# Order of the last chunks, last units and first units in a two-block transformer kernel

## The chip, the cores and the metric

The kernel runs on one core of a Trainium2 chip. TensorE (PE) multiplies matrices into PSUM; VectorE (DVE), ScalarE (ACT) and GpSimd (POOL) compute on SBUF, the first two on PSUM too; SyncE (SP) here only issues DMAs. Each engine runs its own instructions in order, and they wait for one another by semaphores. The metric is the time on the device in microseconds (us), the median of the runs.

## The reference

Two transformer blocks over 1024 tokens of width 1024, all in float32. The first has a Fourier branch and softmax attention. The second, on which the change bears, has stick-breaking attention, a causal convolution, gates and a gated feed-forward part:

```python
h = rms_norm(x, norm_mix_pre)
proj = h @ w_in                                  # values v are 512 of its columns
...
x = x + rms_norm(merged @ w_out, norm_mix_post)  # the second output projection
h = rms_norm(x, norm_ffn_pre)
u = causal_dwconv(h @ w_up, conv_ffn_w)          # 1024 -> 2 x 2816
a, g = split(u)
f = (gelu(g) * a) @ w_down                       # 2816 -> 1024, the down projection
out = x + rms_norm(f, norm_ffn_post)
```

## The kernel before

Precision comes from splitting each float32 operand into a high part in the fast fp32r format and a low part, the rest. The helper three (L672 to L676) issues the three matmuls high x high, high x low and low x high, each 128x128 by 512 columns.

**Weights.** They come in chunks of 128x1024, in the order of the constants C_V2, C_OUT2, C_UP, C_DOWN. SyncE loads a chunk into one of two staging slots (w_staging). GpSimd splits it (split, L559 to L570: two operations for the high part, L566 and L567, one for the low part, L569) into one of the four slots of w_ring, and raises w_split. It may do so once the chunk that held the slot four chunks before is used; TensorE raises w_used for that behind its last matmul with a chunk.

**Token-major units** (tm_units, L688). A unit is one tile of 128 tokens by 512 columns; it runs over chunks times two steps of the contraction, 24 matmuls in all for four chunks. The first lead units are interleaved chunk by chunk, the last two as well, the others run one after another. before(u) adds waits, after(u) adds the eight transposes of a normalised tile. For the values (T_V2) lead is 1, and behind units 0 to 3 tiles 4 to 7 of the block's input are transposed. For the second half of the second output projection (T_OUT2 + TT) lead is 2, and behind unit u stand the transposes of tile u - 3. ScalarE copies the high part out of PSUM (L1560), VectorE subtracts to get the low part (L1917) and raises nt_free. Then the up projection starts with the first token half: it waits for the tiles 0 to 3, and for the copies of all units (tm_free).

**Down projection.** The gated product (ffn_mid, FFT) has 22 feature tiles (FT), one for each weight chunk. All eight banks of PSUM hold the sums of four token tiles by 1024 columns, so the tokens are done in two halves of four tiles, and each half runs over its 22 chunks. For each chunk ScalarE makes the high part of 128x512 (mid_hi, L1819), VectorE the low part (mid_lo, L2378), into one of two slots of ffn_split (FS); a slot is free once the chunk two before is used. TensorE's down() does six matmuls for each token tile, 24 a chunk. In the last chunk each tile raises dn_mm (the last one w_used), ScalarE and VectorE copy its 1024 columns to ffn_out (Y2; L1863 and L2412), and half 1 may use the banks again. Then finish() does the root mean square, for each tile: square (L1832) and a first guess of the inverse root on ScalarE, its refinement (L1891 to L1894), scaling by gain (L2389) and the addition of the residual (L2392) on VectorE; ScalarE stores the tile (L1837) and loads the residual of the tile two on (L1827). For half 0 these steps stand between mid_hi and mid_lo of half 1's chunks 2 to 7, in both engines' order. For half 1 they come behind the copies of all four tiles.

Of the kernel before, what the change touches and what calls it, by code (L numbers as in the profile page):

```python
# [22 lines left out]
F32R = mybir.dt.float32r  # L23
# [4 lines left out]
P = 128  # L28
D = 1024
# [229 lines left out]
def two_block_kernel(nc, a, const, scratch, out):  # L259
    ctx = ExitStack()  # L260
    with ctx:
# [133 lines left out]
        FS = at("ffn_split", [P, 2, 2, N_TOK], R1, F32R)[:, :, :, 0:FW]  # L395
        Y2 = at("ffn_out", [P, 4, D], R1 + 4096)
# [266 lines left out]
        def _(pe):  # L663
# [24 lines left out]
            def tm_units(t0, units, c0, chunks, ncols, stat, before=None, after=None, follows=False, lead=1):  # L688
# [326 lines left out]
            tm_units(T_V2, TT, C_V2, 4, FW, a2_stat, follows=True,  # L1015
# [134 lines left out]
            tm_units(T_OUT2 + TT, TT, C_OUT2 + 4, 4, FW, mr_stat, follows=True, lead=2,  # L1150
# [39 lines left out]
            for half in range(2):  # L1190
                def down(j, s, first=False, last=False):
# [5 lines left out]
                    for t in ((2, 3, 0, 1) if first and not half else range(4)):  # L1197
# [6 lines left out]
                        for g in range(2):  # L1204
                            ins = three(PB[:, 2 * t + g, :], sh, sl, WR[:, r, 0, FW * g:FW * (g + 1)],
                                        WR[:, r, 1, FW * g:FW * (g + 1)], first, last)
                        if last and t < 3:
                            ins.then_inc(S["dn_mm"], 1)
# [7 lines left out]
                for s in range(FT - 4, FT):  # L1216
                    down(s, s, last=s == FT - 1)
# [3 lines left out]
        def _(act):  # L1221
# [625 lines left out]
            for half in range(2):  # L1847
                if half:
                    mid_hi(1, 1, 1)
                    for s in range(6):  # L1850
                        if s < 5:
                            finish(0, s)
                        mid_hi(1, s + 2, s % 2)
                with act.Fori(4 if half else 1, FT // 2) as i:
                    for s in range(2):
                        mid_hi(half, i * 2 + s, s)
                if half:
                    act.wait_ge(S["f_stored"], 64)
                else:
                    mid_hi(1, 0, 0)  # L1860
                for t in range(4):
                    down_ready(act, half, t)
                    act.activation(Y2[:, t, 0:FW], PB[:, 2 * t, :], ACT.Copy).then_inc(S["dn_ya"], 1)  # L1863
                act.wait_ge(S["dn_ya"], 4 * half + 4)
                act.wait_ge(S["dn_yv"], 4 * half + 4)
            for s in range(5):
                finish(1, s)

            act.wait_ge(S["f_stored"], 16 * TT)
# [3 lines left out]
        def _(v):  # L1873
# [519 lines left out]

            v.wait_ge(S["gains3_in"], 16)
            v.wait_ge(S["up_f"], FT + 1)
            for half in range(2):
                if half:
                    mid_lo(1, 1, 1)
                    for s in range(6):
                        if 1 <= s < 5:  # L2400
                            finish(0, s - 1)
                        mid_lo(1, s + 2, s % 2)
                with v.Fori(4 if half else 1, FT // 2) as i:
                    for s in range(2):
                        mid_lo(half, i * 2 + s, s)
# [106 lines left out]
```

## Time and profile before

| | us |
|---|---|
| runs before | 2164.91, 2169.05, 2169.08; median 2169.05 |
| profiled execution | 2165.13 |
| its span, first to last instruction | 2162.9 |
| TensorE busy | 2091.7 (97%) |
| VectorE busy | 1086.4 (50%) |
| ScalarE busy | 828.9 (38%) |
| GpSimd busy | 747.1 (35%) |
| mean granted clock of TensorE | 0.991 of 2.4 GHz |

The span is what the trace covers; the 2.2 us around it belong to the execution's time. Busy shares are means over all stages. The down projection runs from about 1890 to 2144, the second output projection ends at 1388, the values units run from 611 to 664. A row of the timeline is one instruction with its start, its length, its engine and line, what it writes and reads, and in brackets how long the engine had been idle before it and who ended that.

### The profile page before, as it was taken

To read this page: it belongs to the slowest core of one execution; us is meant where nothing else is said; L and a number is where in the kernel's file an instruction comes from. 1 tells how busy PE (TensorE), PEld (TensorE's weight loads), DVE (VectorE), ACT (ScalarE), POOL (GpSimd) and SP (SyncE) were. 2 spreads that over 40 slices of the span, in tenths; PEclk is the share of its full clock that TensorE was granted. 3 is DMA by queue.
4 is the path that set the end of the run, shared out by engine and by line. 5 is a ranking of instruction groups with operands and counts; after the bars stand their busy time and mean duration, and the time that the engine had idled before them with its cause. 6 is when DMAs were issued, how large, how long until landed. Compare 5 with 4: busy or idle time off the path is not lost.

```text
span 2162.9 us, 27982 instructions
## 1 busy us (share of the span) xinstructions
PE 2091.7 (97%) x10634; PEld 1742.7 (81%) x10634; DVE 1086.4 (50%) x1576; ACT 828.9 (38%) x1482; POOL 747.1 (35%) x661
## 2 busy tenths in 40 slices
PE   8999999999999999999999999999999999999996
PEld 7988889998877787778877888778888888878785
DVE  6565678885261666667576650722223222221613
ACT  4342279995242555645455321522212221111212
POOL 2532422222234222223221444043333333367672
PEclk9999999999999999999999999999999999999998
DMA  5211210101322111112112533321111111132432
GB/s 168 61 49 68 69 57 11 47 11 50 112 99 59 51 63 54 63 43 74 52 47 106 193 126 108 137 59 49 48 48 48 48 40 47 48 117 97 155 98 78
DMA packets 144683, 159.91 MB, mean 74 GB/s; under 512 B 6939, under 2 KB 112951, under 8 KB 144583
## 3 DMA queue, kind: packets, MB, share of 16 engines
q1 hardware_dynamic: 121319, 97.45, 14.8%
q10 hardware_dynamic: 23264, 61.10, 8.0%
q8 instruction: 67, 1.10, 0.2%
q14 instruction: 33, 0.27, 0.0%
HBM read 129.16 MB, written 29.36 MB: 73 GB/s over the span
## 4 chain that ended last, share of the span: by engine, by line
PE 84%; DVE 7%; issue 5%; ACT 2%; POOL 1%; DMA 1%; ACTq 0%; DVEq 0%; POOLq 0%
PE psum L674 18%; PE psum L676 17%; PE psum L675 17%; PE psum L1035 15%; PE psum L931 3%; PE psum L943 3%; PE psum L1072 1%; PE psum L962 1%; PE psum L963 1%; PE psum L964 1%; DVE softplus_part L2231 1%; PE psum L1056 1%; PE psum L684 1%; PE psum L1057 1%; PE psum L1089 1%
## 5 line engine op out<-in xcount | busy, mean ns | idle before, releaser
L566 POOL TENSOR_TENSOR w_ring<-w_staging,zero 128x8 fp32r<-128x8 f32 x172 | 43.4, 252 | 1187.3 <-PE psum L676 705.2
L569 POOL TENSOR_TENSOR w_ring<-w_staging,w_ring 128x1024 fp32r<-128x1024 f32 (+1 forms) x172 | 445.7, 2591 | 14.4
L1035 PE MATMUL psum<-h,w_ring 128*128 128x512 f32 x1728 | 434.1, 401 | 0.7 <-ACT v L1565 0.7
L1035 PEld LDWEIGHTS psum<-h,w_ring 128*128 128x128 f32 x1728 | 317.5, 190 | 67.9 <-ACT v L1565 1.1
L674 PE MATMUL psum<-ffn_in,w_ring 128*128 128x512 f32 x672 | 265.4, 395 | 0.0
L676 PE MATMUL psum<-ffn_in,w_ring 128*128 128x512 f32 x672 | 264.2, 393 | 0.0
L675 PE MATMUL psum<-ffn_in,w_ring 128*128 128x512 f32 x672 | 263.8, 393 | 0.0
L2364 DVE SCALAR_TENSOR_TENSOR up_buf<-psum,vectors,up_buf 128x1023 f32<-128x1023 f32 x44 | 56.4, 1283 | 309.8 <-ACT up_buf L1808 309.8
L567 POOL TENSOR_SCALAR w_ring<-w_staging 128x1016 fp32r<-128x1016 f32 (+1 forms) x172 | 184.3, 1071 | 0.0
L1808 ACT ACTIVATE up_buf<-psum,vectors 128x1024 f32<-128x1024 f32 x44 | 49.2, 1117 | 268.0 <-PE psum L676 267.9
L676 PEld LDWEIGHTS psum<-ffn_in,w_ring 128*128 128x128 f32 x672 | 126.0, 188 | 30.5
L675 PEld LDWEIGHTS psum<-ffn_in,w_ring 128*128 128x128 f32 x672 | 126.3, 188 | 29.3
L674 PEld LDWEIGHTS psum<-ffn_in,w_ring 128*128 128x128 f32 x672 | 126.0, 188 | 29.0
L674 PE MATMUL psum<-w_ring,ffn_split 128*128 128x512 f32 x352 | 140.7, 400 | 4.9 <-DVE ffn_split L2378 4.9
L676 PE MATMUL psum<-w_ring,ffn_split 128*128 128x512 f32 x352 | 139.9, 397 | 0.0
L675 PE MATMUL psum<-w_ring,ffn_split 128*128 128x512 f32 x352 | 139.7, 397 | 0.0
L2378 DVE TENSOR_TENSOR ffn_split<-ffn_mid,ffn_split 128x512 fp32r<-128x512 f32 x44 | 45.0, 1025 | 174.2 <-ACT ffn_split L1819 169.3
L2243 DVE TENSOR_TENSOR stick_w_t<-psum,stick_w_t 128x512 fp32r<-128x512 f32 (+3 forms) x96 | 53.4, 556 | 111.9 <-ACT stick_w_t L1642 111.9
L1819 ACT ACTIVATE ffn_split<-ffn_mid 128x512 fp32r (+1 forms) x44 | 27.7, 632 | 202.3 <-PE psum L676 184.6
L2231 DVE TENSOR_TENSOR_SCAN softplus_part<-one,softplus 128x128 f32<-128x128 f32 (+7 forms) x64 | 97.6, 1525 | 2.2
L1642 ACT ACTIVATE stick_w_t<-psum 128x512 fp32r<-128x512 f32 (+3 forms) x96 | 47.1, 491 | 130.5 <-PE psum L1072 129.3
L1520 ACT ACTIVATE probs<-psum,minus_max 128x348 f32<-128x348 f32 x192 | 91.6, 551 | 2.3 <-DVE minus_max L2157 1.9
(286 smaller groups left out, 4543.2 us busy)
## 6 DMA issues: line engine op xcount, KB each, us to landing
w_staging<-in_w_in SPq DMA_DIRECT2D x58, 512.0 KB, 3.8
w_staging<-in_w_up SPq DMA_DIRECT2D x44, 512.0 KB, 3.8
w_staging<-in_w_down SPq DMA_DIRECT2D x44, 512.0 KB, 3.3
w_staging<-in_w_out SPq DMA_DIRECT2D x16, 512.0 KB, 3.8
scratch_gates<-gate_out ACTq DMA_DIRECT2D x32, 256.0 KB, 2.3
merge_gates<-scratch_gates ACTq DMA_DIRECT2D x16, 512.0 KB, 4.5
x_again<-scratch_x ACTq DMA_DIRECT2D x16, 512.0 KB, 4.4
x_again<-in_x ACTq DMA_DIRECT2D x16, 256.0 KB, 2.7
```

The source lines that it names most:

```text
L567: pool.tensor_scalar(hi[:, 0:w], WS[:, s, 0:w], 1.0, 0.0, ALU.mult, ALU.add).then_inc(S["w_hi"], 1)
L569: pool.tensor_tensor(lo[:, 0:width], WS[:, s, 0:width], plain(hi[:, 0:width]), ALU.subtract).then_inc(S["w_split"], 1)
L674: pe.matmul(dst, sh, mh, start=first, stop=False)
L675: pe.matmul(dst, sh, ml, start=False, stop=False)
L676: return pe.matmul(dst, sl, mh, start=False, stop=last)
L931: ins = pe.matmul(PB[:, b, 0:KPART], QS[:, h, P * t:P * t + P], k2[:, h // GROUP, KPART * b:KPART * (b + 1)], start=x == 0, stop=x == 1)
L943: ins = pe.transpose(PB[0:rows, 3 + g, P * (kt % 4):P * (kt % 4) + P], PR[:, i % 2, first:first + rows], IDENT[:, :])
L1035: ins = pe.matmul(mix_bank(h), (sl if x == 2 else sh)[:, P * k:P * k + P], ml if x == 1 else mh, start=m == 0, stop=m == UNIT // 2 - 1)
L1520: act.activation(PR[:, i % 2, KPART * b:KPART * (b + 1)], PB[:, b, 0:KPART], ACT.Exp, bias=NB[:, i % 2:i % 2 + 1], scale=-1.0).then_inc(S[ ...
L2231: link(v.tensor_tensor_scan(ZL[:, i % 2, n - 1::-1], ONE[:, 0:1].broadcast_to([P, n]), ZS[:, i % 3, n - 1::-1], 0.0, ALU.mult, ALU.add))
L2243: v.tensor_tensor(WT[:, 1, 4 * g:4 * g + w, cols], PB[:, 4, 0:P * w].rearrange("p (k n) -> p k n", n=P), plain(WT[:, 0, 4 * g:4 * g + w, c ...
L2364: v.scalar_tensor_tensor(out=UB[:, g, 1:N_TOK], in0=up[:, 0:N_TOK - 1], scalar=w1, in1=UB[:, g, 1:N_TOK], op0=ALU.mult, op1=ALU.add).then_ ...
```

## The change

In tm_units a flag paired=False runs the last two units one after another too; the second half of the second output projection uses it. The values units get lead=2.

In the down projection the last four chunks (18 to 21) of each half run tile by tile: all four chunks for token tile 0, then for tile 1, and so on. Their high and low parts go to a buffer of their own, ffn_split_last (FSL), with a slot for each of the four. dn_mm is raised after each tile's four chunks; w_used of the four chunks only within tile 3. The copies and finish() of half 0 stand tile by tile (copy, then finish), and chunks 0 and 1 of half 1 have their parts made before the first of them. In half 1 nothing is copied: ScalarE squares straight from PSUM (pair(t)), VectorE scales straight from PSUM, and the last tile is scaled, added and stored in two halves of 512 columns.

```diff
+        FSL = at("ffn_split_last", [P, 4, 2, FW], R1 + 12288, F32R)
...
-            def tm_units(t0, units, c0, chunks, ncols, stat, before=None, after=None, follows=False, lead=1):
+            def tm_units(t0, units, c0, chunks, ncols, stat, before=None, after=None, follows=False, lead=1,
+                         paired=True):
...
-                for u in range(lead, units - 2):
+                for u in range(lead, units - 2 if paired else units):
                     for j in range(chunks):
                         part(u, j)
                     if after is not None:
                         after(u)
+                if not paired:
+                    return
...
-            tm_units(T_V2, TT, C_V2, 4, FW, a2_stat, follows=True,
+            tm_units(T_V2, TT, C_V2, 4, FW, a2_stat, follows=True, lead=2,
...
-            tm_units(T_OUT2 + TT, TT, C_OUT2 + 4, 4, FW, mr_stat, follows=True, lead=2,
+            tm_units(T_OUT2 + TT, TT, C_OUT2 + 4, 4, FW, mr_stat, follows=True, lead=2, paired=False,
...
-                for s in range(FT - 4, FT):
-                    down(s, s, last=s == FT - 1)
+                c = C_DOWN + FT * half
+                for t in range(4):
+                    for s in range(FT - 4, FT):
+                        if t == 0:
+                            pe.wait_ge(S["w_split"], c + s + 1)
+                            pe.wait_ge(S["dn_lo"], FT * half + s + 1)
+                        r = (c + s) % 4
+                        sh, sl = (FSL[:, s - FT + 4, x, P * t:P * t + P] for x in range(2))
+                        for g in range(2):
+                            ins = three(PB[:, 2 * t + g, :], sh, sl, WR[:, r, 0, FW * g:FW * (g + 1)],
+                                        WR[:, r, 1, FW * g:FW * (g + 1)], False, s == FT - 1)
+                        if t == 3:
+                            ins.then_inc(S["w_used"], 1)
+                        elif s == FT - 1:
+                            ins.then_inc(S["dn_mm"], 1)
...
             def mid_hi(half, j, s):
-                if half or not isinstance(j, int) or j >= 2:
+                if not isinstance(j, int):
                     act.wait_ge(S["w_used"], j + (C_DOWN + FT * half - 1))
+                elif half:
+                    act.wait_ge(S["w_used"], C_DOWN + FT - 4 + j - 1)
...
+            def last_hi(half, j):
+                if half:
+                    act.wait_ge(S["w_used"], C_DOWN + FT)
+                act.activation(FSL[:, j - FT + 4, 0, :], FFT[:, j, FW * half:FW * half + FW], ACT.Copy).then_inc(S["dn_hi"], 1)
...
+            with act.Fori(1, FT // 2 - 2) as i:
+                for s in range(2):
+                    mid_hi(0, i * 2 + s, s)
+            for j in range(FT - 4, FT):
+                last_hi(0, j)
+            mid_hi(1, 0, 0)
+            mid_hi(1, 1, 1)
+            for t in range(4):
+                down_ready(act, 0, t)
+                act.activation(Y2[:, t, 0:FW], PB[:, 2 * t, :], ACT.Copy).then_inc(S["dn_ya"], 1)
+                act.wait_ge(S["dn_ya"], t + 1)
+                act.wait_ge(S["dn_yv"], t + 1)
+                finish(0, t)
+            finish(0, 4)
...
+            for t in range(4):
+                down_ready(act, 1, t)
+                link(act.activation(JUNK3[:, :], pair(t), ACT.Square, accum_out=SS[:, t:t + 1]))
+                guess(P, t, 1, 1.0 / D, False)
+                if t:
+                    m = 4 + t - 1
+                    act.wait_ge(S["f_out"], m + 1)
+                    act.dma_start(out[0, P * m:P * m + P, :], Y2[:, t - 1, :]).then_inc(S["f_stored"], 16)
+                    if m + 2 < TT:
+                        load_x2(m + 2)
+            for h in range(2):
+                cols = slice(FW * h, FW * h + FW)
+                act.wait_ge(S["f_out"], TT + h)
+                act.dma_start(out[0, N_TOK - P:N_TOK, cols], Y2[:, 3, cols]).then_inc(S["f_stored"], 16)
...
+            with v.Fori(1, FT // 2 - 2) as i:
+                for s in range(2):
+                    mid_lo(0, i * 2 + s, s)
+            for j in range(FT - 4, FT):
+                last_lo(0, j)
+            mid_lo(1, 0, 0)
+            mid_lo(1, 1, 1)
+            for t in range(4):
+                down_ready(v, 0, t)
+                v.tensor_copy(Y2[:, t, FW:D], PB[:, 2 * t + 1, :]).then_inc(S["dn_yv"], 1)
+                finish(0, t)
...
+            v.wait_ge(S["f_stored"], 64)
+            for t in range(4):
+                m = 4 + t
+                refine(P, t, 1, 1.0 / D, RSTD)
+                for h in range(2 if t == 3 else 1):
+                    cols = slice(FW * h, FW * h + FW) if t == 3 else slice(0, D)
+                    link(v.scalar_tensor_tensor(out=Y2[:, t, cols], in0=pair(t)[:, cols], scalar=RSTD[:, t:t + 1],
+                                                in1=GL[:, cols], op0=ALU.mult, op1=ALU.mult))
+                    if h == 0:
+                        v.wait_ge(S[f"xf_in{m % 2}"], 16 * (m // 2 + 1))
+                    v.tensor_tensor(Y2[:, t, cols], Y2[:, t, cols], XF[:, m % 2, cols], ALU.add).then_inc(S["f_out"], 1)
```

The flag last of down() and the loops that stood there before on ScalarE and VectorE, described above, are taken out.

## Rows read from the trace of the kernel before

**Rows 1.** Page, busy time: us, share of the span, instructions.

```profile
PE 2091.7 (97%) x10634; PEld 1742.7 (81%) x10634; DVE 1086.4 (50%) x1576; ACT 828.9 (38%) x1482; POOL 747.1 (35%) x661
```

**Rows 2.** Timeline, values units: start us, us, engine, operation, [idle before, releaser].

```profile
615.63 0.50 PE L674 MATMUL psum<-w_ring,h 128*128 128x512 f32 x1 [1.75 <-POOL w_ring L569]
...
616.83 2.35 POOL L569 TENSOR_TENSOR w_ring<-w_staging,w_ring 128x1024 fp32r<-128x1024 f32 x1
...
619.23 0.50 PE L674 MATMUL psum<-w_ring,h 128*128 128x512 f32 x1 [1.93 <-POOL w_ring L569]
...
621.97 1.22 DVE L1917 TENSOR_TENSOR h<-psum,h 128x1024 fp32r<-128x1024 f32 x1
```

**Rows 3.** Timeline, end of the second output projection.

```profile
1386.49 0.60 ACT L1768 ACTIVATE mix_out<-psum 128x512 f32<-128x512 f32 x1 [5.21 <-PE psum L676]
...
1387.70 1.91 PE L684 MATMUL psum<-ident,xn 128*128 128x128 f32 x16
...
1389.89 1.22 DVE L1917 TENSOR_TENSOR ffn_in<-psum,ffn_in 128x1024 fp32r<-128x1024 f32 x1 [4.18 <-ACT ffn_in L1560]
...
1391.95 0.47 PE L674 MATMUL psum<-ffn_in,w_side 128*128 128x512 f32 x1 [2.34 <-DVE ffn_in L1917]
```

**Rows 4.** Stretches: busy us by engine, granted clock (PEclk), DMA share, GB/s.

```profile
616.00:621.00 5.00, 3.07 (x15) 2.18 (x14) 4.93 (x5) 0.11 (x1) 3.09 (x2) 1.00 0.44 126
...
1393.40:1396.80 3.40, 3.40 (x10) 2.60 (x9) 3.40 (x3) 2.26 (x5) 0.00 (x0) 0.51 0.39 153
...
2042.00:2045.40 3.40, 3.40 (x10) 2.62 (x9) 2.32 (x2) 0.00 (x0) 0.00 (x0) 0.50 0.54 192
```

**Rows 5.** Timeline, boundary of the down projection's halves.

```profile
2014.29 0.40 PE L674 MATMUL psum<-w_ring,ffn_split 128*128 128x512 f32 x1
...
2033.65 3.34 DVE L2392 TENSOR_TENSOR ffn_out<-ffn_out,x_again 128x1024 f32<-128x1024 f32 x1
...
2038.56 2.70 DVE L2378 TENSOR_TENSOR ffn_split<-ffn_mid,ffn_split 128x512 fp32r<-128x512 f32 x1 [1.57 <-ACT ffn_split L1819]
...
2041.32 0.50 PE L674 MATMUL psum<-w_ring,ffn_split 128*128 128x512 f32 x1 [4.31 <-DVE ffn_split L2378]
```

**Rows 6.** Timeline, VectorE beside back-to-back splits of weights.

```profile
607.65 3.51 DVE L2198 SCALAR_TENSOR_TENSOR h<-h,rstd_x,final_gain 128x1024 f32<-128x1024 f32 x1
...
607.69 2.39 POOL L569 TENSOR_TENSOR w_ring<-w_staging,w_ring 128x1024 fp32r<-128x1024 f32 x1
```

**Rows 7.** Timeline, steady chunks of the down projection, half 1.

```profile
2110.63 0.63 ACT L1819 ACTIVATE ffn_split<-ffn_mid 128x512 fp32r x1 [5.03 <-PE psum L676]
...
2116.13 0.20 POOL L566 TENSOR_TENSOR w_ring<-w_staging,zero 128x8 fp32r<-128x8 f32 x1 [1.58 <-PE psum L676]
...
2117.43 2.74 POOL L569 TENSOR_TENSOR w_ring<-w_staging,w_ring 128x1024 fp32r<-128x1024 f32 x1
...
2133.08 0.63 ACT L1819 ACTIVATE ffn_split<-ffn_mid 128x512 fp32r x1 [5.03 <-PE psum L676]
```

**Rows 8.** Timeline, the tail behind the last matmul.

```profile
2143.76 0.40 PE L676 MATMUL psum<-w_ring,ffn_split 128*128 128x512 f32 x1
...
2144.19 0.69 DVE L2412 COPY ffn_out<-psum 128x512 f32<-128x512 f32 x1 [0.72 <-PE psum L676]
...
2146.63 0.15 DVE L1891 TENSOR_SCALAR mean<-sumsq 128x1 f32<-128x1 f32 x1 [1.74 <-ACT rsqrt_guess L1249]
...
2147.27 1.28 DVE L2389 SCALAR_TENSOR_TENSOR ffn_out<-ffn_out,rstd,last_gain 128x1024 f32<-128x1024 f32 x1
...
2158.62 1.23 DVE L2392 TENSOR_TENSOR ffn_out<-ffn_out,x_again 128x1024 f32<-128x1024 f32 x1 [0.78 <-DMA x_again<-scratch_x]
```

**Rows 9.** DMA view, issues: count, KB each, median us to landing.

```profile
scratch_gates<-gate_out ACTq DMA_DIRECT2D x32, 256.0 KB, 2.3
...
x_again<-scratch_x ACTq DMA_DIRECT2D x16, 512.0 KB, 4.4
...
out<-ffn_out ACTq DMA_DIRECT2D x8, 512.0 KB, 3.0
```

More of the change, by code:

```diff
@@ L1190, in _, with down @@
             for half in range(2):
-                def down(j, s, first=False, last=False):
+                def down(j, s, first=False):
                     c = C_DOWN + FT * half
@@ L1205, in down @@
                             ins = three(PB[:, 2 * t + g, :], sh, sl, WR[:, r, 0, FW * g:FW * (g + 1)],
-                                        WR[:, r, 1, FW * g:FW * (g + 1)], first, last)
-                        if last and t < 3:
-                            ins.then_inc(S["dn_mm"], 1)
+                                        WR[:, r, 1, FW * g:FW * (g + 1)], first, False)
                     ins.then_inc(S["w_used"], 1)
@@ L1846, in _ @@
             load_x2(1)
[L1847 to L1865, printed above, removed]
@@ L1866, in _ @@
-            for s in range(5):
-                finish(1, s)
-            act.wait_ge(S["f_stored"], 16 * TT)
+            with act.Fori(1, FT // 2 - 2) as i:
[11 more added lines that the diff above has]
+                finish(0, t)
@@ new lines, in _ @@
+            finish(0, 4)
+            with act.Fori(1, FT // 2 - 2) as i:
+                for s in range(2):
+                    mid_hi(1, i * 2 + s, s)
+            for j in range(FT - 4, FT):
+                last_hi(1, j)
+            for t in range(4):
[8 more added lines that the diff above has]
+                        load_x2(m + 2)
@@ L1872, in _ @@
+            for h in range(2):
+                cols = slice(FW * h, FW * h + FW)
+                act.wait_ge(S["f_out"], TT + h)
+                act.dma_start(out[0, N_TOK - P:N_TOK, cols], Y2[:, 3, cols]).then_inc(S["f_stored"], 16)
+            act.wait_ge(S["f_stored"], 16 * (TT + 1))
         @block.vector
@@ L2392, in finish, with last_lo @@
                 v.tensor_tensor(Y2[:, s, :], Y2[:, s, :], XF[:, m % 2, :], ALU.add).then_inc(S["f_out"], 1)
+            def last_lo(half, j):
+                v.wait_ge(S["dn_hi"], FT * half + j + 1)
+                v.tensor_tensor(FSL[:, j - FT + 4, 1, :], FFT[:, j, FW * half:FW * half + FW],
+                                plain(FSL[:, j - FT + 4, 0, :]), ALU.subtract).then_inc(S["dn_lo"], 1)
             v.wait_ge(S["gains3_in"], 16)
             v.wait_ge(S["up_f"], FT + 1)
[L2396 to L2405, printed above, removed]
-                if half:
-                    v.wait_ge(S["f_stored"], 64)
-                else:
-                    mid_lo(1, 0, 0)
-                for t in range(4):
-                    down_ready(v, half, t)
-                    v.tensor_copy(Y2[:, t, FW:D], PB[:, 2 * t + 1, :]).then_inc(S["dn_yv"], 1)
@@ L2413, in _ @@
-            for s in range(4):
-                finish(1, s)
+            with v.Fori(1, FT // 2 - 2) as i:
+                for s in range(2):
+                    mid_lo(0, i * 2 + s, s)
+            for j in range(FT - 4, FT):
+                last_lo(0, j)
[5 more added lines that the diff above has]
+                finish(0, t)
@@ new lines, in _ @@
+            with v.Fori(1, FT // 2 - 2) as i:
+                for s in range(2):
+                    mid_lo(1, i * 2 + s, s)
+            for j in range(FT - 4, FT):
+                last_lo(1, j)
+            v.wait_ge(S["f_stored"], 64)
[9 more added lines that the diff above has]
+                    v.tensor_tensor(Y2[:, t, cols], Y2[:, t, cols], XF[:, m % 2, cols], ALU.add).then_inc(S["f_out"], 1)
```

## The prediction

> **What bounds the kernel now.** Read the page first: TensorE is busy 97% of the span and at full clock nearly throughout [rows 1]. So an edit pays only where TensorE stands still, or after its last matmul. The timeline of TensorE, searched for starts more than 0.26 us apart, shows where: two waits in the first values unit [rows 2], one ahead of the up projection [rows 3], one in the second half of the down projection [rows 5], and the tail [rows 8]. The change touches all four.
>
> A unit of 24 matmuls, or one chunk of the down projection, takes 5.61 us: four chunks lie between the two hi copies of [rows 7], (2133.08 - 2110.63) / 4. Six matmuls take 1.40 us.
>
> **Values units.** Unit 0 reads its four weight chunks as GpSimd splits them and waits for the third and fourth, 1.75 and 1.93 us; with the matmul that starts late behind each wait, it ends 4.2 us later than a unit without waits [rows 2]. With lead=2 each chunk serves two units, 2.8 us instead of 1.4, so the fourth chunk is wanted at about 619.3; its split ends at 616.83 + 2.35 = 619.18. Both waits go. What is late next: transposes of tiles 4 and 5 now stand together behind units 0 and 1, at 622.2, and tile 5 needs VectorE's subtraction for tile 3, which starts at 621.97 and ends at 623.19: 0.2 to 0.4 us of wait. GpSimd and VectorE aren't moved by this edit, and the units' last slots are released as before. **Gain 3.8** (3.4 to 4.1).
>
> **Second output projection.** Units 6 and 7 interleaved end 1.4 us apart, the copy of unit 6 starts at 1386.49, the transposes of tiles 3 and 4 at 1387.70, and the up projection waits 2.34 us for VectorE's half of tile 3 [rows 3]. The stretch behind the wait runs at a granted clock of 0.51, that is 1.2 GHz [rows 4]: some eight matmuls at 0.43 instead of 0.23 us, 1.5 us. In sequence unit 6 ends 4.2 us earlier (5.61 - 1.40), tile 3 is transposed ahead of unit 7, and its subtraction, at 1389.89 today, comes before unit 7 is through, at 1387.70 plus the 0.9 us of eight transposes. The other condition, the copy of unit 7, starts 0.43 us behind the unit's last matmul as in [rows 8], takes 0.6 and ends near 1389.7, just as the transposes of tile 4 do. So the up projection starts near 1389.9 instead of 1391.95, and at 2.4 GHz: 2.05 + 1.5. The slots of the four chunks are released later by up to 4 us, but the next split waits for the last normalised tile (the test at C_UP + 2 in GpSimd's loop) anyway. The next wait, in front of the second token half, hangs on TensorE's own transposes and moves along. **Gain 3.6** (2.0 if the clock falls anyway, 4.0 at most).
>
> **The tail.** Now: last matmul starts at 2143.76, both engines copy at 2144.19, the mean is read at 2146.63, the scaling starts at 2147.27, and four tiles are then finished in a row on VectorE; the last add ends at 2159.85 [rows 8], the store lands and the span ends at 2162.9: 18.7 us behind the last copy's start. After: three of the four tiles are finished under the last tiles' matmuls (4.9 us of work each, 5.61 us of cover; if that cover were gone, each would cost VectorE's 2.5 us again). Behind the last matmul: the square starts 0.8 us earlier, straight from PSUM, so the scaling starts at 2146.5; on halves of 512 columns the scaling and the add cost about 0.7 us each, what the copy of 512 columns takes [rows 8], so the second half is ready at 2149.35. A 512 KB store lands in 3.0 us, a 256 KB one in 2.3 [rows 9]; of today's 3.05 from the last add to the span's end I leave 2.65, and the two ends make 0.4 either way. New end 2152.0. The residual of the last tile, late by 0.78 us today, is loaded one tile earlier; with 4.4 us [rows 9] it is there 1 us before the add. **Gain 10.9** (10.3 to 11.3).
>
> **The boundary of the two halves.** Today TensorE loses there: 4.31 us of idle time for one low half [rows 5], then the stretch at 0.50 clock [rows 4], 1.4, and some 0.2 of late starts: 6.0 in all. The matmuls from 2014.29 [rows 5] to 2143.76 [rows 8] take 129.7 us where 22 chunks need 123.5. The change takes these waits away: tiles 0 to 2 of half 0 are copied and finished under half 0's own matmuls. But it sets new ones, because all four ring slots of the last chunks are held until tile 3. I count from T, the start of chunk 18 in half 0.
> - Chunk 21 is split after chunk 17 is used: released at T + 0.24, 4.0 us long (2116.13 to 2120.17, [rows 7]), against TensorE's want at T + 4.2. About 0.3 lost, with the late start.
> - Tiles 0 and 1: copy at T + 6.1 and 11.7, VectorE through at 11.7 and 17.4, with GpSimd idle.
> - The next split, half 1's chunk 0, is released at T + 18.8, by tile 3's first six matmuls. It ends at 22.5, TensorE wants it at 22.7. But then the slots of three more chunks are free, and GpSimd splits without a pause until T + 34.
> - Two operations that both read SBUF, one on VectorE and one on GpSimd, take turns in this trace: a scaling issued at 607.65 ran 3.51 us instead of 1.28, because a split had begun at 607.69 and held until 610.08 [rows 6]; an add took 3.34 instead of 1.22 [rows 5]. Applied step by step (who issues second waits for the other's end and then needs 1.07, 0.55 or 2.3 us), tile 2 is through at T + 28.0, not 22.6.
> - VectorE copies tile 3 only behind that, at 28.0 to 28.7. TensorE's chunk 0 of half 1 wants these banks at T + 27.0: a stall of 1.75.
> - Tile 3's square starts at 28.8, its VectorE chain runs from 30.4 to 38.4. Queued behind it on ScalarE are the store, the load and the hi copy of chunk 2, then the low half: 1.57 from the add's end to the subtraction's start [rows 5], and 1.2. Ready at T + 41.2, wanted at 35.9: a stall of 5.4.
> - Behind that stall the clock falls once more, 1.5; behind the 1.75 it doesn't (waits of 1.75 and 1.93 us were followed by 1.00 [rows 2, 4]).
> Sum 0.3 + 1.85 + 5.5 + 1.5 = 9.1 against 6.0: **a loss of 3.1**. The bounds are wide: nothing but the 0.3 is lost if the two chains keep clear of the splits (a gain of 5.7), and one more turn of 3.3 us in each chain makes a loss of 8. I take 3.1 because the same walk through today's boundary gives 4.5 us where the trace has 4.3. Half 1's own chunk 21 has no rival on VectorE and costs nothing. The number of matmuls, loads and bytes doesn't change; one store becomes two.
>
> [...]
>
> **Sum.** 3.8 + 3.6 + 10.9 - 3.1 = 15.2 us. The profiled execution took 2165.1 for a span of 2162.9, so 2149.9 by its own. The three runs shown fall at 2164.9 and twice at 2169.1; I don't know what sets the two levels, so I start from their middle, 2167.1, and predict 2152.
>
> **Rivals.**
> - The boundary's stalls hardly come (A): GpSimd's splits fall between VectorE's operations. For it: the turns depend on tenths of a microsecond, and VectorE has 0.6 us to spare in each tile. Against: three splits in a row leave no gap. One to two of the 9.1 us stay, so 7 more are gained: 2145.
> - The boundary is worse (B): a turn of 3.3 us more, and the clock falls behind the first stall too, 1.5: 2157.
> - The early edits don't do what they say (C): the wait for the fourth values chunk only moves to a later matmul, and the up projection still waits for the seventh copy. The slack is 0.1 us in the first case, nearly 0 in the second. It gives 2159.
> - Slower than before (D): the turns don't end with the boundary. GpSimd leaves it three chunks behind and one VectorE subtraction falls into every chunk. The place is the 18 looped chunks of half 1, the price is whatever a split with its turn takes beyond 5.61 us, and it decides from 1.1 us a chunk: 20 us for 18 chunks, more than the gain of 15.2 and the 4.3 of the bound below. Against it: 4.0 us and a turn of 0.6 make 4.6 [rows 5, 7]. It would give 2172.
>
> **How the numbers follow.** Forecast 0.58, A 0.22, B 0.10, C 0.07, D 0.03. The forecast's own spread is 2148 to 2156, by the two levels of the runs and the bounds above. Reaching down to A and up to B the range is 2144 to 2158. A measurement of this kernel can tell about 0.2%, 4.3 us, from no change; only D and the far end of C come near it: faster 0.95, same 0.03, slower 0.02.
>
> **What would show it.** In the profile after: no wait for a split behind the first values chunk; the up projection's first matmul directly behind the transposes, at full clock; in the down projection two stalls of TensorE in half 1, one waiting for the copy at L2412's place at the fourth tile of chunk 0, one for the low half of chunk 2; VectorE operations of 3.3 us beside splits; 8 us from last matmul to the end. Wrong would be: no stall over 2 us in half 1 (A), a slow stretch behind the first (B), or a tail over 9 us.

## The result, and the profile after

The changed kernel takes 2153.85 us (median of four runs, 2152.85 to 2155.09) against 2166.98 for the kernel before (four runs beside it, 2164.04 to 2169.08): a ratio of 0.9946, 95% interval 0.9932 to 0.9960. That is 13.1 us less, by the interval 8.7 to 14.7. The forecast was 2152.0, 15.2 less than 2167.1 (start value and forecast as in the prediction). The profiled execution took 2153.87 for a span of 2151.7 us, 11.2 less than the span before.

The page of the changed kernel, span and busy times by engine, answers to [rows 1]:

```profile
span 2151.7 us, 27966 instructions
PE 2092.1 (97%) x10634; PEld 1742.8 (81%) x10634; DVE 1085.6 (50%) x1574; ACT 826.3 (38%) x1478; POOL 750.0 (35%) x661
```

TensorE is busy for the same time as before. What went is idle time. The shares are still rounded to the same per cents, so the page alone tells nothing of where. For that I cut each trace at the first matmul of a stage and compare the lengths (us):

| kernel | start to values | values to mix | mix to out 2 | out 2 to up | up to down | down to its last matmul | to the end |
|---|---|---|---|---|---|---|---|
| before | 610.84 | 53.39 | 630.91 | 96.81 | 498.03 | 253.78 | 19.14 |
| after | 612.47 | 49.61 | 633.39 | 94.37 | 496.31 | 257.51 | 8.04 |
| difference | +1.6 | -3.8 | +2.5 | -2.4 | -1.7 | +3.7 | -11.1 |

Mix is the attention with its branches between the values units and the second output projection (out 2). Five differences belong to the four terms of the sum (the second output projection has two, out 2 to up and up to down). The other two, at the start and in mix, lie where nothing was changed.

**First values units.** The timeline of TensorE after, its transposes behind units 0 and 1, answers to [rows 2] (start, length, engine and line, output and inputs, and in brackets the idle time before with its releaser):

```profile
623.82 1.04 PE L685 MATMUL psum<-ident,xn 128*128 128x128 f32 x8
625.02 1.06 PE L685 MATMUL psum<-ident,xn 128*128 128x128 f32 x8 [0.16 <-DVE h L1951]
```

No matmul ahead of them waits for a split. The second transposes are late by 0.16 us, where 0.2 to 0.4 was foreseen.

**Before the up projection.** The timeline after, TensorE's transposes and the subtraction of tile 3 on VectorE, answers to [rows 3]:

```profile
1382.47 1.03 PE L685 MATMUL psum<-ident,xn 128*128 128x128 f32 x8
1385.94 1.22 DVE L1951 TENSOR_TENSOR ffn_in<-psum,ffn_in 128x1024 fp32r<-128x1024 f32 x1
1388.94 1.03 PE L685 MATMUL psum<-ident,xn 128*128 128x128 f32 x8
1389.84 0.47 PE L675 MATMUL psum<-ffn_in,w_side 128*128 128x512 f32 x1
```

The subtraction ends at 1387.16, ahead of the last transposes, and the first matmul of the up projection starts 0.90 us after their start, with no idle time. A window of the changed kernel over this first matmul shows that the slow stretch of [rows 4] is gone (length, busy us and count for PE, PEld, DVE, ACT and POOL, granted clock, DMA share, GB/s):

```profile
1389.00:1393.00 4.00, 4.00 (x23) 3.37 (x22) 3.73 (x4) 3.79 (x6) 0.00 (x0) 1.00 0.32 125
```

So the stage after it is shorter by 1.7 us.

**The boundary of the halves.** The timeline after, all three engines, answers to [rows 5]. L567 to L570 are the split on GpSimd, L1928 is the last step of the refinement in finish(), L2423 and L2426 its scaling and its add, L2444 the copy of a tile:

```profile
2006.62 0.20 POOL L567 TENSOR_TENSOR w_ring<-w_staging,zero 128x8 fp32r<-128x8 f32 x1 [14.35 <-PE psum L677]
2008.07 2.29 DVE L1928 SCALAR_TENSOR_TENSOR rstd<-newton_b,rsqrt_guess 128x1 f32<-128x1 f32 x1
2010.40 2.18 DVE L2423 SCALAR_TENSOR_TENSOR ffn_out<-ffn_out,rstd,last_gain 128x1024 f32<-128x1024 f32 x1
2011.60 3.24 POOL L570 TENSOR_TENSOR w_ring<-w_staging,w_ring 128x1024 fp32r<-128x1024 f32 x1
2012.62 3.31 DVE L2426 TENSOR_TENSOR ffn_out<-ffn_out,x_again 128x1024 f32<-128x1024 f32 x1
2015.85 0.68 DVE L2444 COPY ffn_out<-psum 128x512 f32<-128x512 f32 x1
2016.67 0.47 PE L675 MATMUL psum<-w_ring,ffn_split 128*128 128x512 f32 x1 [1.75 <-DVE ffn_out L2444]
2020.72 3.51 DVE L2423 SCALAR_TENSOR_TENSOR ffn_out<-ffn_out,rstd,last_gain 128x1024 f32<-128x1024 f32 x1
2024.26 1.22 DVE L2426 TENSOR_TENSOR ffn_out<-ffn_out,x_again 128x1024 f32<-128x1024 f32 x1
2024.56 0.98 POOL L567 TENSOR_TENSOR w_ring<-w_staging,zero 128x8 fp32r<-128x8 f32 x1 [1.41 <-DMA w_staging<-in_w_down]
2029.59 0.80 PE L675 MATMUL psum<-w_ring,ffn_split 128*128 128x512 f32 x1 [5.68 <-DVE ffn_split L2412]
```

Read it downwards: GpSimd has stood still for 14.35 us and then splits back to back. The finishing of tile 2 meets the splits: a refinement step on 128x1 takes 2.29 us where tile 1's took 0.16, and the two operations of 1.2 us take 2.18 and 3.31. The copy of tile 3 comes late, and TensorE waits 1.75 us. The scaling of tile 3 takes 3.51, the low half of chunk 2 stands behind it, and TensorE waits 5.68 us.

Windows after, in the same columns, behind the first stall, behind the second, and over the whole slow stretch at the second:

```profile
2017.00:2020.00 3.00, 3.00 (x15) 2.42 (x14) 1.66 (x4) 1.18 (x4) 2.92 (x3) 1.00 0.64 247
2030.20:2033.60 3.40, 3.40 (x10) 2.66 (x9) 0.00 (x0) 0.00 (x0) 3.21 (x2) 0.50 0.40 145
2027.30:2034.20 6.90, 4.61 (x11) 3.69 (x12) 2.55 (x2) 0.66 (x2) 6.11 (x4) 0.51 0.55 172
```

TensorE runs at full clock behind the first and at 1.2 GHz behind the second. There the clock is down from 2027.3, 2.3 us before the stall ends, to 2034.2; TensorE works through 4.61 us of that, against 3.40 behind the stall of the kernel before ([rows 4]).

**The tail.** The timeline after, from the last matmul on, answers to [rows 8]:

```profile
2143.66 0.40 PE L677 MATMUL psum<-w_ring,ffn_split_last 128*128 128x512 f32 x1
2144.10 1.02 ACT L1890 ACTIVATE junk<-psum 128x1024 f32<-128x1024 f32 x1 [3.99 <-PE psum L677]
2146.36 0.75 DVE L2457 SCALAR_TENSOR_TENSOR ffn_out<-psum,rstd,last_gain 128x512 f32<-128x512 f32 x1
2148.53 0.69 DVE L2461 TENSOR_TENSOR ffn_out<-ffn_out,x_again 128x512 f32<-128x512 f32 x1
```

The last add ends at 2149.22 and the span at 2151.7.

### The profile page after: what moved, and what is told of

It is laid out like the page before. It is cut to its first block, busy times and chain, and to the rows that moved or that the text cites. A ratio compares the mean times of both kernels' runs of the same rounds, so it can differ in the third digit from the quotient of the medians.

```text
span 2151.7 us, 27966 instructions
## 1 busy us (share of the span) xinstructions
PE 2092.1 (97%) x10634; PEld 1742.8 (81%) x10634; DVE 1085.6 (50%) x1574; ACT 826.3 (38%) x1478; POOL 750.0 (35%) x661
## 4 chain that ended last, share of the span: by engine, by line
PE 85%; DVE 9%; ACT 3%; issue 2%; DMA 1%; ACTq 0%; POOL 0%; SPq 0%; DVEq 0%
PE psum L675 18%; PE psum L677 18%; PE psum L676 18%; PE psum L1039 15%; PE psum L935 3%; PE psum L947 3%; PE psum L1076 1%; PE psum L966 1%; PE psum L967 1%; PE psum L968 1%; DVE softplus_part L2265 1%; PE psum L1060 1%; PE psum L685 1%; PE psum L1061 1%; PE psum L1093 1%
## 5 line engine op out<-in xcount | busy, mean ns | idle before, releaser
L567 POOL TENSOR_TENSOR w_ring<-w_staging,zero 128x8 fp32r<-128x8 f32 x172 | 47.6, 277 | 1184.2 <-PE psum L677 703.2
L570 POOL TENSOR_TENSOR w_ring<-w_staging,w_ring 128x1024 fp32r<-128x1024 f32 (+1 forms) x172 | 444.5, 2584 | 14.4
L675 PE MATMUL psum<-w_ring,ffn_split 128*128 128x512 f32 x288 | 115.6, 401 | 8.0 <-DVE ffn_split L2412 6.3
L677 PE MATMUL psum<-w_ring,ffn_split 128*128 128x512 f32 x288 | 114.7, 398 | 0.0
L676 PE MATMUL psum<-w_ring,ffn_split 128*128 128x512 f32 x288 | 114.6, 398 | 0.0
L2412 DVE TENSOR_TENSOR ffn_split<-ffn_mid,ffn_split 128x512 fp32r<-128x512 f32 x36 | 33.8, 942 | 149.8 <-ACT ffn_split L1836 144.9
L675 PE MATMUL psum<-u,w_ring 128*128 128x260 f32 (+1 forms) x256 | 89.2, 349 | 2.5 <-DVE u L1951 2.5
```

The lines of the kernel that those rows point to most:

```text
L570: pool.tensor_tensor(lo[:, 0:width], WS[:, s, 0:width], plain(hi[:, 0:width]), ALU.subtract).then_inc(S["w_split"], 1)
L675: pe.matmul(dst, sh, mh, start=first, stop=False)
L676: pe.matmul(dst, sh, ml, start=False, stop=False)
L677: return pe.matmul(dst, sl, mh, start=False, stop=last)
```

## The experiments

The theory: the four terms of the sum are separate, and the loss at the boundary comes from GpSimd's splits alone, which take turns with finish() on VectorE. Its rivals are in the expectations: that copies and scalings cost the time by themselves, that order alone would mend it, and, for the time that went missing in mix, that an earlier start of this stage costs.

### e1_values: lead=2 alone, on the kernel before

```diff
-            tm_units(T_V2, TT, C_V2, 4, FW, a2_stat, follows=True,
+            tm_units(T_V2, TT, C_V2, 4, FW, a2_stat, follows=True, lead=2,
```

> The kernel before with one edit, the values units' lead=2. My theory: the stage of the values units gets 3.8 us shorter as forecast, and what follows moves along, apart from the stretches at half clock in the mix stage (stick-breaking attention beside projections), of which there may be one more or one fewer, 1.5 us each: 2163.2 against 2167.0, 2161.5 to 2165. Rival: the earlier start of the mix stage runs into something with a time of its own there, a transfer or a semaphore, and the stage always gives back 2.1 us, as between the two profiles: 2165.3.

Measured 2162.78 (seven runs, 2158.81 to 2165.41) against 2167.88; ratio 0.9978, interval 0.9966 to 0.9989. Values to mix takes 49.75 instead of 53.39: 3.6 us. The medians differ by 5.1, and the runs of e1 spread over 6.6, so the size of the gain rests on the stage. Mix takes 631.76, 0.85 more than before and not the 2.1 of the rival. Up to down takes 496.50 instead of 498.02: the second of two stretches at half clock in that stage is missing here, although the edit doesn't touch it.

### e2_units: paired=False alone, on the kernel before

```diff
...
-                for u in range(lead, units - 2):
+                for u in range(lead, units - 2 if paired else units):
...
+                if not paired:
+                    return
...
-            tm_units(T_OUT2 + TT, TT, C_OUT2 + 4, 4, FW, mr_stat, follows=True, lead=2,
+            tm_units(T_OUT2 + TT, TT, C_OUT2 + 4, 4, FW, mr_stat, follows=True, lead=2, paired=False,
```

> The kernel before with one edit, the last two units of the second output projection in sequence. My theory: the wait of 2.34 us and the slow stretch behind it go, 3.6 to 4.0 us, and nothing comes back in the up projection, which runs without a gap: 2163.2. Rival: the clock falls at the second wait of the up projection all the more, or the third and fourth chunks' splits come late: 2165.5.

Measured 2164.00 (ten runs, 2162.70 to 2165.72), ratio 0.9982, interval 0.9973 to 0.9992: 3.9 us. By stage: out 2 to up 94.38 and up to down 496.52, that is 2.4 and 1.5 less.

This run held something else. Its values units are those of the kernel before, but the stage took 55.05 us instead of 53.39. The timeline of e2, the wait that [rows 2] has for the kernel before, and a window behind it:

```profile
619.64 0.50 PE L674 MATMUL psum<-w_ring,h 128*128 128x512 f32 x1 [1.93 <-POOL w_ring L569]
620.00:623.40 3.40, 3.40 (x13) 2.80 (x12) 3.40 (x4) 1.69 (x3) 0.00 (x0) 0.52 0.56 169
```

The window of the kernel before at the same place:

```profile
619.50:622.90 3.40, 3.40 (x20) 2.86 (x20) 3.40 (x4) 1.61 (x3) 0.00 (x0) 1.00 0.54 155
```

The same wait of 1.93 us is followed by 1.2 GHz in one execution and by 2.4 GHz in the other.

### e3_half1_only: half 0 in its old order, half 1 tile by tile

```diff
-            with act.Fori(1, FT // 2 - 2) as i:
+            with act.Fori(1, FT // 2) as i:
                 for s in range(2):
                     mid_hi(0, i * 2 + s, s)
-            for j in range(FT - 4, FT):
-                last_hi(0, j)
             mid_hi(1, 0, 0)
-            mid_hi(1, 1, 1)
             for t in range(4):
...
-                finish(0, t)
-            finish(0, 4)
-            with act.Fori(1, FT // 2 - 2) as i:
+            act.wait_ge(S["dn_ya"], 4)
+            act.wait_ge(S["dn_yv"], 4)
+            mid_hi(1, 1, 1)
+            for s in range(6):
+                if s < 5:
+                    finish(0, s)
+                mid_hi(1, s + 2, s % 2)
+            with act.Fori(4, FT // 2 - 2) as i:
```

VectorE and TensorE follow in the same way, and mid_hi() waits as in the kernel before.

> The changed kernel, but half 0 of the down projection ends and is finished in the order of before; half 1 keeps the tile-by-tile order. My theory: the boundary loses 6.0 us again instead of 9.9, the tail keeps its 11.1: 3.9 faster than the changed kernel, 2150.0. Rival: the boundary's loss isn't due to half 0's order but to half 1's tile order or to what DMA moves there: it stays at 9.9, and the time at 2153.9.

Measured 2147.35 (four runs, 2146.66 to 2148.76), ratio 0.9905, interval 0.9889 to 0.9922. The timeline of e3 has the one stall of the kernel before again, and nothing else at the boundary:

```profile
2033.67 0.80 PE L675 MATMUL psum<-w_ring,ffn_split 128*128 128x512 f32 x1 [4.32 <-DVE ffn_split L2415]
```

Down to its last matmul is 253.99, 3.5 less than after; to the end 7.98. So the tail's gain comes from half 1 alone, and half 0's new order is a loss of 3.5 us by itself. The run is 2.6 us better than expected. In its profiled execution (2146.66) the mix stage took 629.42, 4.0 less than after (below, e8); the other runs have no trace.

### e4_thin_splits: the cause taken away

The splits of half 1's first four chunks cover 16 of the 1024 columns; the rest of these weights isn't made.

```diff
+                if thin:
+                    width = 16
...
-            run(C_UP + 4, C_END, 1)
+            run(C_UP + 4, C_DOWN + FT, 1)
+            run(C_DOWN + FT, C_DOWN + FT + 4, 1, True)
+            run(C_DOWN + FT + 4, C_END, 1)
```

> The changed kernel, where GpSimd splits only 16 of the 1024 columns of half 1's first four weight chunks, so the rest of these four chunks keeps what the slots held (part of the computation is left out). Waits and order stay. My theory: VectorE's finishing chains then run at their undisturbed pace, 3.2 us instead of 7 to 8; the stall for the copy of tile 3 and the one for the low half of chunk 2 both vanish, with the slow stretch behind: 9.4 us off, 2144.5. Rival: the chains are late by their order alone, or by ScalarE's issues, and not by GpSimd: the stalls stay within 2 us of what they are, 2152 or more.

Measured 2143.28 (four runs, 2140.86 to 2144.26), ratio 0.9886, interval 0.9869 to 0.9902. Down to its last matmul takes 247.76, 9.75 less than after, with no stall at the boundary. The timeline of e4, VectorE: scaling and add of tile 2, copy of tile 3, scaling and add of tile 3:

```profile
2005.16 1.28 DVE L2427 SCALAR_TENSOR_TENSOR ffn_out<-ffn_out,rstd,last_gain 128x1024 f32<-128x1024 f32 x1
2006.48 1.22 DVE L2430 TENSOR_TENSOR ffn_out<-ffn_out,x_again 128x1024 f32<-128x1024 f32 x1
2007.70 0.69 DVE L2448 COPY ffn_out<-psum 128x512 f32<-128x512 f32 x1
2010.78 1.28 DVE L2427 SCALAR_TENSOR_TENSOR ffn_out<-ffn_out,rstd,last_gain 128x1024 f32<-128x1024 f32 x1
2012.10 1.26 DVE L2430 TENSOR_TENSOR ffn_out<-ffn_out,x_again 128x1024 f32<-128x1024 f32 x1
```

Without the splits tile 2's scaling and add take 1.28 and 1.22 us in place of 2.18 and 3.31 after, and tile 3's scaling 1.28 in place of 3.51. Both stalls and the slow stretch hang on the splits. That the order of the copies costs by itself is refuted: it is the same here.

### e5_spare: the wait kept away instead

The high and low parts of half 1's chunks 2 and 3 are made before the copies, into spare columns (FSX), and VectorE copies tiles 2 and 3 before it finishes either.

```diff
+        FSX = at("ffn_split_spare", [P, 2, 2, N_TOK], R1, F32R)[:, :, :, FW:N_TOK]
...
+                if half:
+                    down(2, 2, fs=FSX)
+                    down(3, 3, fs=FSX)
+                    down(4, 4)
+                    down(5, 5)
+                with pe.Fori(half, (FT - 4) // 4) as i:
...
+            for j in range(2):
+                act.activation(FSX[:, j, 0, :], FFT[:, j + 2, FW:N_TOK], ACT.Copy).then_inc(S["dn_hi"], 1)
...
-                finish(0, t)
-            with v.Fori(1, FT // 2 - 2) as i:
+                if t < 2:
+                    finish(0, t)
+            finish(0, 2)
+            finish(0, 3)
+            with v.Fori(2, FT // 2 - 2) as i:
```

> The changed kernel with two more edits at the boundary of the halves: the high and low parts of half 1's chunks 2 and 3 are made ahead of the boundary, in the unused columns of ffn_split, and VectorE copies tile 3 ahead of finishing tiles 2 and 3. My theory: both stalls are waits for VectorE work that stands behind a finishing chain slowed by the splits; with the copy ahead of it and the low parts made early, nobody waits for these chains, however slow. Only the 0.3 us for chunk 21's split stay of the 9.9: 9.6 off, 2144.3. Rival: the chains take so long that chunk 4's low half is late instead (the walk gives it 22 us from the boundary, the two chains need 17), and the stall only moves, 3 us or more and a slow stretch: 2149 or more.

Measured 2143.46 (five runs, 2141.6 to 2144.6) against 2164.69 (ten runs); ratio 0.9895, interval 0.9879 to 0.9912. It is the fastest complete kernel of this study, 21.2 us under the kernel before. The timeline of e5, VectorE:

```profile
2011.71 0.69 DVE L2456 COPY ffn_out<-psum 128x512 f32<-128x512 f32 x1 [4.89 <-PE psum L678]
2015.19 2.02 DVE L2431 SCALAR_TENSOR_TENSOR ffn_out<-ffn_out,rstd,last_gain 128x1024 f32<-128x1024 f32 x1
2017.25 3.35 DVE L2434 TENSOR_TENSOR ffn_out<-ffn_out,x_again 128x1024 f32<-128x1024 f32 x1
2021.89 3.33 DVE L2431 SCALAR_TENSOR_TENSOR ffn_out<-ffn_out,rstd,last_gain 128x1024 f32<-128x1024 f32 x1
2025.26 2.10 DVE L2434 TENSOR_TENSOR ffn_out<-ffn_out,x_again 128x1024 f32<-128x1024 f32 x1
```

The window 2010 to 2035 of e5:

```profile
2010.00:2035.00 25.00, 25.00 (x109) 20.07 (x108) 16.16 (x14) 3.42 (x7) 23.86 (x18) 1.00 0.68 220
```

The same window after:

```profile
2010.00:2035.00 25.00, 17.57 (x66) 13.52 (x65) 16.08 (x12) 3.31 (x7) 21.67 (x16) 0.86 0.61 208
```

The turns are as long as after, 10.80 us for the four operations on tiles 2 and 3 against 10.22, where e4 needs 1.28 and 1.26 for a tile. But TensorE has what it needs and runs through: 25.00 busy of 25.00. The stage takes 247.56. The rival, chunk 4's low half late instead, didn't come. The first half of the edit alone, the spare columns without the earlier copy, was not run.

### e6_copies_first: the second half of e5's edit alone

```diff
-                finish(0, t)
+                if t < 2:
+                    finish(0, t)
+            finish(0, 2)
+            finish(0, 3)
```

> The changed kernel, where VectorE copies tile 3 ahead of finishing tiles 2 and 3; nothing else. My theory, walked through step by step: the 1.75 us stall goes, but both chains now run one after another beside three splits in a row, and the low half of chunk 2 comes 11 us late instead of 5.7: 3.6 slower than the changed kernel, 2157.4. Rival: the copy's place is what was wrong, and the 1.85 us of the first stall are simply gained: 2152.

Measured 2153.15 (four runs, 2151.11 to 2154.24), ratio 0.9944, interval 0.9925 to 0.9963. The timeline of e6 has one stall:

```profile
2027.50 0.80 PE L675 MATMUL psum<-w_ring,ffn_split 128*128 128x512 f32 x1 [7.59 <-DVE ffn_split L2412]
```

The first stall is gone, and the second is longer by 1.9 us, what the first had cost. By its time alone the run would fit a rival with 2152 too; the trace decides. So a copy put ahead saves nothing in stalls while the low half of chunk 2 still stands behind both chains. The time was not as expected: 3.6 us slower was said, and 2153.15 is no slower than the changed kernel's 2153.85 (1.3 above e8's 2151.88, within the spread of the runs). Down to its last matmul is 256.52, even 1.0 shorter than after, mostly because fewer matmuls behind the one stall run at half clock. The longer second stall came, but the walk gave 11 us for it, one turn of 3.3 more than the chip, where a scaling got in just ahead of a split's step (start 2012.06 and 1.28 us, the step 2012.22 and 2.03 us instead of 1.04).

### e7_shift: where the mix stage starts

Sixteen matmuls of no use before mix, on the changed kernel, bring its start back to the kernel before's distance from the values units:

```diff
+            for _ in range(16):
+                pe.matmul(PB[:, 0, :], A2[:, 0, 0, 0:P], A2[:, 0, 0, 0:FW], start=True, stop=True)
             mix(AHEAD)
```

> The changed kernel with 16 matmuls of 128x512 more ahead of the mix stage, 16 x 0.23 = 3.7 us, so that everything behind comes that much later. My theory: the mix stage has the same waits of up to 2.3 us at the same places in every run, and which of them are followed by a stretch at half clock depends on when they fall; so the stage takes 626.3 us plus 1.6 for each such stretch, two to four of them, whatever the shift, and the kernel takes 2153.9 + 3.7, give or take 1.6 for each stretch: 2154 to 2160. Rival: the stage is longer in the changed kernel because it starts earlier against something that has a time of its own; put back by 3.7 us it takes 630.9 again as in the kernel before, and 2.1 us of the shift come back.

Measured 2153.86 (three runs, 2153.57 to 2156.23), ratio 0.9950, interval 0.9932 to 0.9968. Values to mix takes 53.38, mix 630.48. By itself this speaks for the rival as well as against it, so one more run had to decide. The time lies just under the expected 2154 to 2160. Part of it is that up to down takes 494.89, where after has 496.32: this profile alone has no stretch at half clock in that stage. The timeline after has one near 1407; the window of e7:

```profile
1386.00:1420.00 34.00, 31.37 (x152) 25.73 (x151) 19.85 (x27) 14.13 (x23) 11.86 (x11) 1.00 0.33 107
```

### e8_same_again: the changed kernel once more

No edit.

> The changed kernel, unchanged, profiled once more. My theory: the part before the values units differs by up to 1.6 us with the arrival of the first inputs, and the number of slow stretches in the mix stage is not fixed by the code: another count than four is likely, and the stage then differs from 633.4 by 1.6 a stretch. Rival: the same code takes the same 633.4 us in this stage, within 0.3.

Measured 2151.88 (two runs, 2150.84 and 2152.92), ratio 0.9937, interval 0.9912 to 0.9961. Its mix stage takes 631.36, the same code in the first profile 633.39. The windows of the mix stage tell why. After, first profile:

```profile
715.00:720.00 5.00, 4.29 (x13) 3.43 (x14) 4.13 (x7) 2.71 (x4) 0.00 (x0) 0.66 0.36 105
960.00:965.00 5.00, 3.65 (x11) 2.92 (x12) 4.77 (x9) 2.28 (x4) 0.29 (x1) 0.74 0.37 105
1010.00:1015.00 5.00, 5.00 (x18) 4.24 (x18) 3.86 (x5) 3.60 (x5) 0.12 (x1) 0.66 0.40 116
1140.00:1145.00 5.00, 5.00 (x19) 4.21 (x18) 3.85 (x5) 3.45 (x5) 0.00 (x0) 0.67 0.40 123
```

The same code again, e8:

```profile
715.00:720.00 5.00, 4.40 (x23) 3.73 (x24) 4.06 (x6) 3.00 (x5) 0.00 (x0) 1.00 0.36 105
960.00:965.00 5.00, 5.00 (x17) 3.93 (x16) 3.60 (x6) 2.01 (x4) 0.00 (x0) 0.66 0.35 103
1005.00:1015.00 10.00, 8.11 (x31) 6.39 (x31) 8.67 (x9) 5.17 (x7) 3.52 (x1) 0.83 0.26 81
1135.00:1145.00 10.00, 7.36 (x29) 5.74 (x28) 8.67 (x9) 4.75 (x6) 0.34 (x2) 0.83 0.70 251
```

One place, near 717 us, is at full clock in e8 and partly at half clock in the first profile; the other three have a stretch in both. The trace before has three such stretches in this stage, near 717, 1140 and 882, the last in this window:

```profile
880.00:885.00 5.00, 4.44 (x15) 3.78 (x16) 3.74 (x6) 4.10 (x5) 0.00 (x0) 0.66 0.01 3
```

Counted so over all ten profiles: two stretches in e3, mix 629.42; three in before, e1, e2, e4, e6, e7 and e8, 630.48 to 631.76; four in after and e5, 633.39 and 632.84. By these lengths a stretch costs 1.8 to 1.9 us in this stage, and which waits are followed by one differs from run to run. e1, which starts mix as early as the changed kernel does, has 631.76. That the earlier start costs 2.1 us every time is refuted by e8 and e1. Two things may still hang on the start: with three stretches, the profiles that start mix early (e1, e4, e6, e8) have 631.28 to 631.76, the others (before, e2, e7) 630.48 to 631.24; and the stretch near 882 us is found only in before and in e7, the two with 53.4 us from values to mix. Why the count was four in the first profile isn't settled. (e8's down stage, 258.51, is 1.0 us longer than after's. The two stalls are as before, 1.75 and 5.72; but TensorE waits 1.88 us for the first low half of half 0, at 1897.46, and 0.58 in the first profile.)

## Why the prediction was right

- **Values units**: -3.8 forecast, -3.8 measured (-3.6 in e1). The slack of 0.1 us for the fourth chunk sufficed, so C's first condition didn't come.
- **Second output projection**: -3.6 forecast, 4.0 at most; measured 2.4 + 1.7 = 4.1 after, 3.9 in e2. The slow stretch is worth 1.5 to 1.7. The difference is the wait itself: 2.4 instead of 2.05.
- **Tail**: -10.9 forecast, -11.1 measured, and the same in e3 (7.98 to the end) and in all others with half 1's new order. Square at 2144.10, scaling at 2146.36 and last add's end at 2149.22 against 2149.35; the store and the end took 2.5 where I left 2.65.
- **Boundary**: +3.1 forecast, +3.7 measured. The steps came as walked: late starts of 0.22 us for chunk 21's split (0.3); a stall of 1.75 for the copy of tile 3 (1.75); one of 5.68 for the low half of chunk 2 (5.4); the clock down behind the second only. By the distances from start to start beyond 0.23 us, both sides of the change lose more than I said, 10.2 against 9.1 after and 6.3 against 6.0 before. Under-sized was above all the slow stretch, 2.2 us where the sum has 1.5: I took it as long as before's, and TensorE ran through 4.61 us of it. Its length isn't fixed by the stall: behind the stall of 4.32 us in e3 TensorE runs 5.03 us at half clock (window 2031.8 to 2038.7), behind the same one before 3.40. The stall for the copy cost 2.0 with the late matmul behind it (1.85), the one for the low half 5.8 (5.5).
- **What wasn't in the walk**: GpSimd waited 1.41 us at 2024.56 for a staging load. In this pause the add at 2024.26 got in and took 1.22, not 3.3 us. That the second stall still fits, 5.68 against 5.4, is partly luck: counted from T (1988.03 after), tile 3's chain was through at 37.5 and not at 38.4, but the low half's subtraction started 2.11 us behind the add (walk: 1.57) and took 1.94 (1.2), a split beside it. e6, walked in the same way, had a stall of 7.59 against the walk's 11. A walk by turns had the right places; a single turn can be wrong by 2 to 3 us. It isn't noise: after, e7 and e8 have the same turns within 0.06 us, and stalls of 1.75, 1.75, 1.75 and 5.68, 5.73, 5.72.
- **Who waits.** The walk's rule was that the one who issues second waits. By the recorded starts [rows 6] already doesn't say so: the scaling starts at 607.65, 0.04 us ahead of the split, and takes 3.51. So does the one at 2020.72 after, with the split at 2020.76. Within some hundredths of a microsecond the starts don't tell who waits.
- **Outside the sum**: +2.5 in mix, by e8 mostly the number of slow stretches, and +1.6 at the start. The first transposes in the timeline of the kernel before:

```profile
11.49 3.41 PE L684 MATMUL psum<-ident,xn 128*128 128x128 f32 x16 [1.51 <-DVE xn L1933]
```

The same after:

```profile
12.84 3.68 PE L685 MATMUL psum<-ident,xn 128*128 128x128 f32 x16 [3.18 <-DVE xn L1967]
```

Over the ten profiles this stage took 610.84 to 613.70 us, 611.08 in e4 and 613.70 in e5, though no edit touches it. The four terms sum to -15.3, and these two stages give 4.1 of it back: hence 11.2 in the spans. In medians the change is worth 13.1, and 12.8 beside e8 (2151.88 against 2164.69). So both times the gain was some 2 us under the 15.2 of the sum. e8's time is nearer to the forecast than the first one's only because the kernel before was faster beside it, too. The start value of 2167.1, the middle of two levels without an explanation, came within 0.2 us of the median of 2166.98; that was luck.

One reason in the prediction was wrong without moving the time. I took it from two waits of 1.75 and 1.93 us that a wait of this length leaves the clock up. e2 shows the same wait of 1.93 us followed by a clock of 0.52. The value for the stall of 1.75 us was right in this execution, and in e7 and e8 too the clock stayed up there; but the rows it was taken from didn't show that it must, since the wait of 1.93 us has two outcomes some 1.6 us apart (55.05 and 53.39 for the stage). The Trainium skill, "TensorE: Matmul & The Clock Gate", section "HAM oscillation — how this bites in real kernels", tells of a kernel that waits 3 to 5 us for a DMA between its groups of matmuls, and has the clock thrown back every time. The waits of 4.3 to 7.6 us here agree, with 0.50 behind each (0.50 after, 0.51 in e6's window 2023.7 to 2030.6). Its example has no waits as short as 1.75 to 2.34 us: here 2.34 was followed by 0.51 [rows 4], 1.93 by 0.52 or 1.00, and 1.75 by 1.00.

## What to carry to other kernels

When an order holds many buffers and frees them all at once, ask what the waiting engine does next: here GpSimd, idle for 14.35 us, split almost without a pause and made VectorE's two-input operations on 128x1024 in SBUF up to 2.8 times as long, and those on 128x1 of the refinement up to 2.4 us. The remedy wasn't to shorten the chain but to make what TensorE wants next ahead of it, in spare space (e5: the chains as slow as ever, no stall); moving only one of two waits ahead saved no stall (e6). And compare stage by stage: 4.1 us of this result were hidden by stages that nobody touched.

## What the runs showed of the hardware

- **Turns between VectorE and GpSimd.** Where they had to wait for a split, scaling and add of 128x1024 in SBUF took 1.94 (e6) to 3.52 us (e8), without splits (e4) 1.22 to 1.28. It goes both ways: beside the add at 2024.26 after, the split's first step took 0.98 us instead of 0.20. The copies out of PSUM took 0.68 to 0.69 in both cases, and a step with one input in SBUF (L1925, 2018.27 after) 0.15, with a split running. The Trainium skill, "SBUF — State Buffer", section "🔬 SBUF: two separate sides", tells of a lock between the two engines when VectorE's operation has two inputs in SBUF and GpSimd's reads SBUF: whichever starts first holds it for its whole instruction. The lengths agree; who started first doesn't, in the two places where the recorded starts are 0.04 us apart (607.65 before, 2020.72 after).
- **The clock isn't a function of the code.** Identical code had three or four half-clock stretches in the same stage (after and e8), and three at partly other places (before near 717, 882 and 1141, e2 near 965, 1013 and 1142), 1.6 to 1.9 us each. The prediction didn't allow for that. It would explain part of why runs of the kernel before lie between 2162.7 and 2172.0, since two or three stretches more are 3 to 5 us. Their stretches weren't counted, but the mean granted clock on record for each run points the same way: 0.994 for the run of 2162.72, 0.989 for those of 2167.11, 2170.07 and 2171.99.
